# Decay inputs joined to the first z slot of a mixer, with low halves and roundings moved around the normalization before it

## The reference, cut to what matters

```
h = rms_norm_2(x, g_mix[i])
proj = h @ w_in[i]
glu_a, glu_b, q, k, v, z, a_in, b_in, gate_a, gate_b = split_cols(proj, IN_SIZES)
qkv = jax.nn.silu(depthwise_conv(jnp.concatenate([q, k, v], axis=-1), qkv_conv_w[i]))
g = -jnp.exp(a_log[i]) * jax.nn.softplus(a_in + dt_bias[i])
beta = jax.nn.sigmoid(b_in)
o_fwd = gated_delta_rule(q, k, v, g[:, :, 0], beta[:, :, 0])
o = rms_norm_2(o_fwd + o_bwd, delta_norm_g[i]) * jax.nn.silu(z)
```

## Time and profile before

| what | before |
|---|---|
| median of 3 runs | 1201.29 us (1198.54 to 1202.06) |
| the profiled execution's own time | 1202.13 us |
| its span in the profile | 1200.3 us |
| PE busy | 1171.7 us, 98% |
| DVE busy | 839.7 us, 70% |
| ACT busy | 701.5 us, 58% |
| POOL busy | 324.8 us, 27% |
| mean granted TensorE clock | 0.992 |
| HBM read | 197.33 MB |

### The profile page before, as it was taken

How to read it: one execution, slowest core, us unless ns; L and a number is a source line. 1 busy time by engine, 2 the same in 40 slices (tenths; PEclk the granted TensorE clock), 3 DMA queues, 4 the chain that set the end, 5 groups by cost and what they waited for, 6 DMA issues and landing times.

```text
span 1200.3 us, 21345 instructions
## 1 busy us (share of the span) xinstructions
PE 1171.7 (98%) x8592; PEld 1088.5 (91%) x8592; DVE 839.7 (70%) x1519; ACT 701.5 (58%) x1181; POOL 324.8 (27%) x257
## 2 busy tenths in 40 slices
PE   8999999999999999999999999999999999999997
PEld 7777899998887799998899999999989989999886
DVE  6796588884685578885558787889954656555456
ACT  5466576663467676664466667667666445444344
POOL 1172300000028300000156666675555220000010
PEclk9999999999999999999979999999999999999999
DMA  7633355546553366555333332332223646555542
GB/s 286 252 141 141 125 210 210 184 181 216 176 178 139 124 244 211 202 188 211 141 137 118 132 111 104 140 109 102 105 72 108 226 176 222 209 186 201 203 154 81
DMA packets 31587, 199.74 MB, mean 166 GB/s; under 512 B 4289, under 2 KB 6481, under 8 KB 8706
## 3 DMA queue, kind: packets, MB, share of 16 engines
q1 hardware_dynamic: 29506, 189.27, 44.1%
q0 software_dynamic: 1840, 8.60, 1.9%
q10 hardware_dynamic: 144, 0.52, 0.1%
HBM read 197.33 MB, written 1.05 MB: 165 GB/s over the span
## 4 chain that ended last, share of the span: by engine, by line
PE 85%; DVE 7%; ACT 3%; issue 2%; POOL 1%; DMA 1%; SPq 0%; POOLq 0%; ACTq 0%; DVEq 0%
PE ps L1190 24%; PE ps L1192 23%; PE ps L1191 23%; PE ps L1567 2%; PE ps L1583 1%; PE ps L1344 1%; PE ps L1363 1%; DVE conv L2773 1%; PE ps L1331 1%; DVE wlo L2387 1%; PE ps L1215 1%; DVE ps L2842 1%; PE ps L1284 1%; PE ps L1197 1%; DVE x L2516 1%
## 5 line engine op out<-in xcount | busy, mean ns | idle before, releaser
L1190 PE MATMUL ps<-halves,whi 128*128 128x256 f32 x1472 | 410.7, 279 | 0.1
L1191 PE MATMUL ps<-halves,whi 128*128 128x256 f32 x1472 | 405.7, 276 | 0.0
L1192 PE MATMUL ps<-halves,wlo 128*128 128x256 f32 x1472 | 405.6, 276 | 0.0
L2387 DVE TENSOR_TENSOR wlo<-raw,whi 128x2048 fp32r<-128x2048 f32 (+1 forms) x133 | 300.7, 2263 | 116.1 <-ACT whi L1847 112.9
L1847 ACT ACTIVATE whi<-raw 128x2048 fp32r<-128x2048 f32 (+1 forms) x143 | 269.3, 1885 | 95.6 <-PE ps L1192 91.4
L1190 PEld LDWEIGHTS ps<-halves,whi 128*128 128x128 f32 x1472 | 283.3, 192 | 0.8 <-DVE halves L2981 0.5
L1192 PEld LDWEIGHTS ps<-halves,wlo 128*128 128x128 f32 x1472 | 283.4, 193 | 0.0
L1191 PEld LDWEIGHTS ps<-halves,whi 128*128 128x128 f32 x1472 | 283.4, 193 | 0.1
L1114 POOL TENSOR_TENSOR wlo<-raw,whi 128x1024 fp32r<-128x1024 f32 x72 | 172.4, 2404 | 54.5 <-ACT whi L1856 53.9
L1006 POOL TENSOR_TENSOR rstd<-sumsq,half_power 128x1 f32<-128x1 f32 x14 | 11.5, 823 | 573.9 <-ACT xn L1874 406.4
L1190 PE MATMUL ps<-whi,halves 128*128 128x512 f32 (+4 forms) x440 | 149.1, 339 | 3.6 <-DVE halves L2490 2.7
(11 more groups left out here) (337 smaller groups left out, 1849.3 us busy)
## 6 DMA issues: line engine op xcount, KB each, us to landing
raw<-in_stream SPq DMA_DIRECT2D x176, 1024.0 KB, 4.8
gain<-in_gains POOLq DMA_DIRECT2D x7, 512.0 KB, 5.6
bias<-in_rel POOLq DMA_DIRECT2D x1, 1536.0 KB, 8.5
raw<-in_stream SPq DMA_DIRECT2D x2, 648.0 KB, 7.9
cst<-in_consts POOLq DMA_DIRECT2D x1, 1280.5 KB, 8.9
raw<-in_stream SPq DMA_DIRECT2D x2, 528.0 KB, 4.2
x<-in_x SPq DMA_DIRECT2D x2, 512.0 KB, 4.6
out<-xn SPq DMA_DIRECT2D x4, 256.0 KB, 2.4
```

The costliest lines, as they stand in the source:

```text
L1190: nc.tensor.matmul(out, a_hi, b_hi, start=start, stop=False)
L1191: nc.tensor.matmul(out, a_hi, b_lo, start=False, stop=False)
L1192: return nc.tensor.matmul(out, a_lo, b_hi, start=False, stop=stop)
L2387: dve.tensor_tensor(used(wlo, n), used(raw, n), used(whi, n).bitcast(F32), ALU.subtract)\
```

## The change

- The slot "ab" and the slot z 0 of round 1 become one matrix of 288 columns (256 of z and the 32 decay columns), stored by rows in two slots of four slices of 128 features each: ("z_decay", 0) and ("z_decay", 1), 128x4x288. The stream has as many slots as before. `ab_products` becomes `first_z_and_decay_products`: the same 48 products with 288 moving columns, into banks 4 and 5 of PSUM.
- Every later z and gates slot of `other` moves up; rounds 1, 2 and 3 keep four slots, round 4 has three.
- z 0 is kept at tick 7 of round 0 (`FIRST_Z_AT`): tanh on ACT, multiplication on DVE (`first_z`). PE's first `level_turn`, which writes bank 4, waits for it.
- Low halves: DVE makes the one of ("z_decay", 0) ahead of tile 0's last normalization; POOL makes the whole one of ("z_decay", 1), where it made half of qk 0's; qk 0's are made behind the normalizations, on POOL behind two memsets, on DVE behind tile 1's `lows`.
- ACT rounds the slot of v 0 (the last of the whole ones) behind tile 1's `round_turned` and no longer ahead of it.
- In round 0 the second half of the slot glu 0 is rounded behind the beginning of the q/k convolution and no longer ahead of it.

```
-    plan.append(("narrow", "ab", ("w_in_2", 0), 6144, 32))
+    rows_major("z_decay", ("w_in_2", 0), [(5120, 2 * P), (6144, 32)])
...
-    other = [glu[0:2], [z[0]] + glu[2:4], [glu[4], z[1]], [z[2], glu[5], z[3]], [glu[6], gates[0]],
+    other = [glu[0:2], glu[2:4] + [z[1]], [glu[4], z[2]], [glu[5], z[3], gates[0]], [glu[6]],
              [glu[7]] + gates[1:2], gates[2:3], gates[3:5]]
...
+FIRST_Z_AT = (0, 7)
...
-        POOL_SLOTS = [slot_of[key] + AHEAD for key, r, tick in MIX_SLOTS if 0 <= r < len(ROUNDS)]
+        POOL_SLOTS = [slot_of[key] + AHEAD for key, r, tick in MIX_SLOTS if 0 <= r < len(ROUNDS)] + [slot_of[("z_decay", 1)]]
...
                 if t == 0:
-                    split_shared(("qk", 0))
+                    n = slot_of[("z_decay", 1)]
+                    pool.wait_ge(*S["weights_high"].at((n, 1)))
+                    pool.tensor_tensor(used(wlo, n), used(raw, n), used(whi, n).bitcast(F32), ALU.subtract)\
+                        .then_inc(*S["pool_weights_low"].one((n, 1)))
 
             pool.memset(sum_row[:, :].bitcast(F32), 0.0).then_inc(*S["rows_cleared"].one("mixer"))
             pool.memset(glu_in[:, :, :], 0.0).then_inc(*S["glu_cleared"].one())
+            split_shared(("qk", 0))
...
+            def first_z_and_decay_products(t):
+
+                for half in range(2):
+                    n = slot_of[("z_decay", half)]
+                    if t == 0:
+                        wait_low(pe, n)
+                    wait_split(5, t, (half,))
+                    wh, wl = used(whi, n), used(wlo, n)
+                    for i in range(4):
+                        kt = 4 * half + i
+                        last = three(ps[:, 4 + t, 0:Z_DECAY], xhi[:, kt, t * P:(t + 1) * P], xlo[:, kt, t * P:(t + 1) * P],
+                                     in_order(wh[:, i, :]), in_order(wl[:, i, :]), kt == 0, kt == KT - 1)
+                    if t:
+                        last.then_inc(*S["weights_used"].one(n))
...
             def level_turn(h):
 
                 pe.wait_ge(*S["inverse_begun"].at(h))
+                if h == 0:
+                    pe.wait_ge(*S["tanh_used"].at(("z", 0)))
...
                 split(last + 3)
                 round_turned(5 if k == 4 else k, [(1, 0), (1, 1)])
+                if k == 4:
+                    split(last + 4)
...
+            def first_z():
+
+                act.wait_ge(*S["weights_used"].at(slot_of[("z_decay", 1)]))
+                act.wait_ge(*tanh_free(TANH_BEFORE[("z", 0)]))
+                act.activation(tanh[:, TANH_OF[("z", 0)], :].rearrange("p (t c) -> p t c", t=2), ps[:, 4:6, 0:2 * P], ACT.Tanh,
+                               scale=0.5).then_inc(*S["tanh_made"].one(("z", 0)))
...
-                    if slot_at(r, i):
+                    if (r, i) == (0, 2):
+                        split_half(slot_of[slot_at(0, 1)] + AHEAD, 1)
+                    if slot_at(r, i) and (r, i) != (0, 1):
                         split_half(slot_of[slot_at(r, i)] + AHEAD, i % 2)
...
                 if k == 4:
                     gain_x(0)
                     scale_x(0)
+                    split(last + 2)
                 normalize(after, [0])
...
                 lows(after, [(1, 0), (1, 1)])
+                if k == 4:
+                    split(last + 3)
...
-                dve.wait_ge(*S["weights_used"].at(slot_of["ab"]))
+                dve.wait_ge(*S["weights_used"].at(slot_of[("z_decay", 1)]))
...
+            def first_z():
+
+                dve.wait_ge(*S["tanh_made"].at(("z", 0)))
+                dve.scalar_tensor_tensor(xn[:, :, 0:TOK], tanh[:, TANH_OF[("z", 0)], :].rearrange("p (t c) -> p t c", t=2), 1.0,
+                                         ps[:, 4:6, 0:2 * P], ALU.add, ALU.mult).then_inc(*S["tanh_used"].one(("z", 0)))
```

More of the change, by code:

```diff
@@ L175, in pack_stream @@
                 out[n].reshape(P, KT, 2 * P)[:] = evens_first(out[n].reshape(P, KT, 2 * P))
-        elif kind == "narrow":
-            a, c = args
-            out[n].reshape(P, KT, 256)[:, :, 0:c] = w[:, a:a + c].reshape(KT, P, c).transpose(1, 0, 2)
         elif kind == "down":
@@ L547 @@
 AB_SPINS = (6, 2)
+Z_DECAY = 2 * P + 32
 END_SPINS = (5, 8)
@@ L556 @@
 NORMS = len(GAINS) - 1
-MIX_SLOTS = [("ab", -1, 0)] + [(slot[0], r, 2 * i) for r, slots in enumerate(ROUNDS) for i, slot in enumerate(slots)] \
+MIX_SLOTS = [(("z", 0), -1, 0)] + [(slot[0], r, 2 * i) for r, slots in enumerate(ROUNDS) for i, slot in enumerate(slots)] \
     + [(("delta_out", i), len(ROUNDS), 0) for i in range(KT // 2)]
@@ L595, in tanh_order @@
                 order.append(key)
+            if (r, i) == FIRST_Z_AT:
+                order.append(("z", 0))
             if r < HEADS and i == 3:
@@ L825, in weights_of @@
                 return at.rearrange("p (k c) -> p k c", k=4)[:, :, 0:sum(c for _, c in entry[3])]
-            if entry[0] == "narrow":
-                return at.rearrange("p (k c) -> p k c", k=KT)[:, :, 0:entry[4]]
             return at
@@ L1452, in half_slot @@
                     last.then_inc(*S["weights_used"].one(n))
-            def ab_products(t):
-                n = slot_of["ab"]
-                if t == 0:
-                    wait_low(pe, n)
-                wh, wl = used(whi, n), used(wlo, n)
-                for kt in range(KT):
-                    if kt % 4 == 0:
-                        wait_split(5, t, (kt // 4,))
-                    last = three(ps[:, 3, t * 32:(t + 1) * 32], xhi[:, kt, t * P:(t + 1) * P], xlo[:, kt, t * P:(t + 1) * P],
-                                 wh[:, kt, :], wl[:, kt, :], kt == 0, kt == KT - 1)
-                if t:
-                    last.then_inc(*S["weights_used"].one(n))
+            def first_z_and_decay_products(t):
[11 more added lines that the diff above has]
+                        last.then_inc(*S["weights_used"].one(n))
             def decay_sums():
@@ L1777, in _ @@
                 turn_norm(5, t)
-                ab_products(t)
+                first_z_and_decay_products(t)
                 if t == 0:
@@ L2301, in _ @@
                         evacuate(finished_slot(r, i))
+                    if (r, i) == FIRST_Z_AT:
+                        first_z()
                     if r < HEADS and i == 3:
@@ L2718, in decay_inputs @@
             def decay_inputs():
-                dve.wait_ge(*S["weights_used"].at(slot_of["ab"]))
+                dve.wait_ge(*S["weights_used"].at(slot_of[("z_decay", 1)]))
                 dve.wait_ge(params2_loaded, 16)
-                link(dve.tensor_copy(ab[:, 0, :, :], ps[:, 3, 0:64].rearrange("p (t c) -> p t c", t=2)))
+                link(dve.tensor_copy(ab[:, 0, :, :], ps[:, 4:6, 2 * P:Z_DECAY]))
                 dt = row_at["dt_bias_2"].unsqueeze(1).broadcast_to([P, TT, 16])
@@ L3032, in _ @@
             decay_inputs()
-            split(slot_of["ab"] + AHEAD)
+            split(slot_of[("z_decay", 1)] + AHEAD)
             for r in range(len(ROUNDS)):
```

## The result

The changed kernel takes 1206.68 us (median of 6 runs, 1205.77 to 1208.56) where the kernel before, on the same chip, takes 1201.5 (6 runs, 1198.54 to 1203.61): a ratio of 1.0047, 95% interval 1.003 to 1.0064. It is slower by 0.5%; the forecast was 1194.0. The profiled execution of the change took 1206.85 us, span 1205.0, against the 1202.13 of before.

The account below looks back on a forecast made before the run. PE, busy 98% of the span, was taken as the bound, with its clock missing only from 600 to 630 us. The terms 0 - 2.7 - 1.9 + 0.6 + 0.3 - 3.5 = -7.2 gave 1194.0 us against the median, range 1190.2 to 1198.8.

Parts of the forecast that it names:

- Part 1: Boundary up to tile 1's transposes: no time won or lost, 0, between -0.7 and +0.5 us.
- Part 4: Head of round 0: ACT becomes later than PE, whose gate wait grows by 0.6 us; ends 0 and +1.0.
- Parts 2 and 3: At full clock, tile 1's turn to the first qk product: -2.7 us; the first qk slot: -1.9 us.
- Part 5: z 0's multiplication enters tick 7 of round 0, where DVE has no gap: +0.3 us, ends 0 and +0.7.
- Part 6: Round 4 has one slot less: -3.5 us; 5.3 if PE alone counted, 2 if DVE holds more.
- A: Rival: the clock falls at the boundary all the same, leaving only round 4's gain; 1198.4 us, chance 0.16.
- B: Rival: DVE holds round 4, which saves 1.5 us instead of 3.5; 1196.0 us, chance 0.12.
- D: Rival: the clock falls about 604, in the second wait, and is slow over round 0's head; 1205.0 us, chance 0.05.

Follow-up runs that it names:

- e3: The changed kernel with POOL's subtraction for ("z_decay", 1) waiting until DVE has normalized tile 0; 1203.26 us.
- e1: The changed kernel with POOL's third subtraction of round 0 waiting until DVE's q/k gate is done; 1200.73 us.
- e4: The changed kernel with POOL waiting both for tile 0's normalization and for the q/k gate; 1198.05 us.
- e2: The changed kernel with ACT again rounding glu 0's second half ahead of the q/k convolution; 1202.95 us.
- e6: The kernel before with only glu 0's second half rounded behind the beginning of the q/k convolution; 1208.08 us.
- e7: The changed kernel with both POOL waits, plus 4 idle PE products in the 1.20 us wait and 4 ahead of the gate's; 1195.47 us.
- e10: The kernel before with 4 idle PE products in the 1.20 us wait and 4 ahead of the gate's wait; 1200.35 us.
- e11: The kernel before with decay products of 256 moving columns and idle PE products in the first wait and ahead of the gate's; 1199.83 us.
- e8: The changed kernel with both POOL waits, gates 1 moved to round 4 in place of glu 6, and glu 6 to round 5; 1198.24 us.
- e5: The kernel before with only the decay products widened, their 32 columns read eight times each; 1201.75 us.
- e9: The changed kernel, POOL left as it is, with 4 idle PE products in the boundary's first wait and 18 ahead of the gate's; 1202.81 us.

## Why the prediction was wrong

Parts 1 and 4 failed: both left out that POOL's subtraction holds DVE, the first between tile 0's turn and tile 1's, the second at the gate. The measured price is 2.08 us at the first, 3.69 at the second, and 4.1 of low clock behind the longer wait.

**Part 1 failed** ("Up to tile 1's transposes: 0"). It put POOL's new subtraction at 2.65 us, "it can start when ACT has rounded, about 594, and ends ahead of 598.8". It began at 594.91, took 3.10 (2.64 in e3, where DVE doesn't normalize beside it) and did end ahead of 598.8, so PE did not wait for it. But the question was not asked what DVE does in that time. Turn to turn of tile 1 took 9.41 us (596.00 to 605.41) where it took 7.83: +1.6 for 0. The earlier trace rows held the hint: L1015 took 0.97 us beside DVE's subtraction and 0.27 without. I read it as a gain on POOL and did not ask for the reverse. The kernel before has a plainer case that no row of the prediction shows: a POOL subtraction of 1024 elements that takes 4.21 us for 2.36, and ends (616.25) 2.2 us behind a DVE subtraction that had begun first and ended at 614.02:

```profile
611.73 2.29 DVE L2387 TENSOR_TENSOR wlo<-raw,whi 128x2048 fp32r<-128x2048 f32 x1
```

```profile
612.04 4.21 POOL L1114 TENSOR_TENSOR wlo<-raw,whi 128x1024 fp32r<-128x1024 f32 x1 [8.83 <-ACT whi L1856]
```

e3 shows the cause.

**Part 4 failed** (+0.6, ends 0 and +1.0; PE's wait at the gate "grows by 0.6"). It compared ACT with PE and left out POOL. The wait is 4.76 us. With POOL behind the gate (e1, e4) it is 1.07, where the part has 0.41 + 0.6; so ACT's side of it was right, and what was missing is that ACT's order decides when POOL runs, and POOL's when DVE may. The part also took a kept clock for granted; the clock fell in this very wait, and that cost 4.1 us more. And it called the new order worth 1.04 us: so it is once POOL is held back (PE waits 1.07 us in e1, 2.02 in e2), but as it stands e6 shows that it costs the kernel before 7 us.

**Parts 2 and 3 were right** where the clock held: from tile 1's turn to the first qk product 5.11 us (605.41 to 610.52) for a forecast 4.95, and the first slot 1.9 us shorter, as forecast. Both gains arrived, and were lost between 617 and 636.

**Part 5 was too small** (+0.3, end +0.7). Where the clock is kept, round 0 from the gate's turn on takes 0.4 more (19.01 in e1, 19.02 in e7; 18.60 before, 18.54 and 18.59 in e10 and e11), which is the place that the part names. But round 1, which loses that multiplication, takes 0.3 more too, in every changed kernel (34.14 to 34.17 for 33.82 to 33.84), and the part has no term for it. What makes it longer stays open.

**Part 6 was right in kind, too large in size**: -3.5 forecast, -2.61 measured. (Its own numbers, 3.76 less 0.42, give 3.34 and not 3.5.) The value from round 6 missed 0.9: at 784.97 PE waits 1.06 us for ACT's cross ratio, which waits for DVE, whose glu 6 multiplication and three taps stand ahead. e8 shows that moving glu 6 only moves it.

**The sum.** Up to the gate the forecast was -4.0 (0, -2.7, -1.9, +0.6); e4 measures -4.30 there. With a kept clock (e7) the marks give -4.30 up to the gate, +0.42 for the rest of round 0, +0.33 for round 1 and -2.58 for round 4: -6.1 for the forecast -7.2. That the first number comes so near is in part luck: tile 1's turn comes 0.5 us sooner behind tile 0's than in the kernel before (7.32 in e4 for 7.83), which part 1 put at 0. The whole time of e7 is 5.6 us below before by the medians, 2.3 to 5.2 by the interval of the ratio. So the forecast described, within a microsecond or some more, the change with two waits of POOL and idle products added, and not the change.

**The rivals.** A (the clock falls at the boundary all the same) did not happen in the profiled execution of the change, but it did in that of e2, which has the same boundary. So A is something that happens in some executions, and its 0.16 says nothing of how often. B was half true (34.05, under its line of 34.5). D came nearest to the outcome, with 1205.0, and had a part of its price, the clock low over round 0's head; but its place (the second wait at 604) and its cause were not these, so the nearness is luck. None of the rivals had POOL against DVE, though the change moves POOL's subtractions.

The Trainium skill ("SBUF — State Buffer", section "Who interferes with whom") states the rule: a DVE instruction with two SBUF inputs and a GpSimd instruction that reads SBUF contend for a shared port pair, and the one that issues first has it for its whole instruction; a DVE instruction with at most one SBUF input, outside the 2-port perf modes, does not contend. The traces agree, instruction by instruction at the gate (see the ends above): `normalize` (x and gain from SBUF) 3.78 us for 1.41, the gate (tanh and conv from SBUF) 4.46 for 0.76 to 0.81; the convolution's taps, one input of which is in PSUM, took 3.21 us for 8 while POOL's subtraction ran, so none of them was held for its 2.4 us. By that rule, read beside the order of POOL, the gate could have been costed, as an estimate: at most one subtraction of 2.36 us ahead of each of its two instructions, 4.7 us; the traces show 3.65 (4.46 for 0.81).

## What to carry to other kernels

When an edit puts a GpSimd instruction of microseconds near the path, write down which DVE instructions with two SBUF inputs start while it runs; each can be held for as long as it lasts, and one wait that puts GpSimd behind them cost nothing that the marks show here (e1, e3), where GpSimd is 27% busy. An order on a third engine (ACT's roundings here) can close the pause in which DVE's short instruction used to run, so its cost is not in its own row. And a gain ahead of a point where another engine is later is no gain until that engine is; e5 moved 3.2 us to the gate and lost them there.

## What the runs showed of the hardware that was not expected

- Two short DVE instructions in a row are each held by one GpSimd instruction when these follow without a pause: the gate's two, 0.8 us of work, took 1.98 and 2.56 us in the change, each until a subtraction of 2.4 us had ended, and 4.46 together in three programs (the change, e3, e6).
- The granted clock differs from execution to execution at the same wait. In executions of e1 alone the mean clock goes from 0.991 (1203.65 us) to 0.998 (1197.19). In the profiled execution of the change waits of 2.01 and 1.23 us at the boundary left the clock at 2.4 GHz; in that of e2 it fell at the end of the same first wait (2.00 us, fall at 598.7). The unchanged wait of 2.13 us at 110 us was followed by 3.4 us at 1.2 GHz in seven profiled executions (the change, e2, e4, e5, e7, e10, e11) and by none in six; tile 0's turn stood at 595.9 to 596.2 us in the seven and at 594.0 to 595.1 in the six.
- Between tile 0's turn and the first qk products the clock fell in all three profiled executions with 32-column products (before, e6, e10) and in one of ten with wide ones (e2). That speaks for the prediction's reading of the earlier trace rows, but what decides a single fall stays open.
- Behind the gate the low stretch was longer where the wait ahead of it was: 10.2 us behind waits of 4.07 to 4.78 (e6, the change, e3), 6.8 behind 2.02 and 1.69 (e2, e5), 3.4 behind 1.07, 1.08 and 0.77 (e4, e8, e9), none behind 1.07, 0.79, 0.41 and 0.18 (e1, e11, before, e7). In the boundary's stretch before the change it was 13.7 us. e1 kept its clock with the waits unfilled, so full clock in e7 and e11 does not show what idle products do.
